# An expert stage whose experts follow one another without a seam: two buffers of split tokens, and prompt tokens turned as full tiles

## The chip, the core and the metric

The kernel runs on one core of one Trainium2 chip. The metric is the device time of one execution in microseconds (us). Three runs of the kernel before gave 3706.44, 3706.96 and 3714.54 us, with a median of 3706.96 us.

The engines are named as in the profile: PE is TensorE (matmuls), PEld its weight loads, DVE is VectorE, ACT is ScalarE, POOL is GpSimd, and SP is the engine that issues most DMAs.

## The reference, cut to what matters

One encoder layer is applied to 512 prompt tokens and 1024 sample tokens with shared weights: a mixer (attention and convolution), and then a mixture of 16 experts in which each expert takes its best tokens. The change touches only the second part:

```python
def expert_choice_ffn(h, w_router, w_gate, w_up, w_down):
    cap = max(1, EC_FACTOR * n // N_EXPERTS)       # 64 prompt, 128 sample tokens
    hf = h.reshape(n, D)
    aff = jax.nn.softmax((hf @ w_router).astype(jnp.float32), axis=-1)
    g, idx = lax.top_k(aff.T, cap)
    xe = hf[idx]
    hid = jax.nn.silu(jnp.einsum('ecd,edf->ecf', xe, w_gate)) * jnp.einsum('ecd,edf->ecf', xe, w_up)
    ye = jnp.einsum('ecf,efd->ecd', hid, w_down) * g[..., None].astype(h.dtype)
    y = jnp.zeros((n, D), h.dtype).at[idx.reshape(-1)].add(ye.reshape(-1, D))
```

Everything is float32. D is 1024, the hidden width of an expert is 2816, which is 22 tiles of 128 rows, and an expert's tokens are 192 columns (64 prompt, 128 sample).

## The kernel before, in words

The function `experts` writes out the work of each engine as its own program. The order on each engine is the order of the code, and semaphores tie the engines together. No planner or scheduler is involved.

To keep float32 accuracy on the fast matmul path, each operand is split into a high part (rounded by ACT) and a low part (the rest, subtracted by DVE). Three products are summed.

**A step.** An expert has 22 steps, one for each tile i of its hidden width. On PE a step is `gate_up(e, i)`: 16 pairs of matmuls (L1204 with the high weights over 384 columns, L1206 with the low weights over 192 columns). With two steps of delay (`BEHIND = 2`) comes `down(e, i-2)`: 10 matmuls of 512 columns (L1221 to L1225), which gather the expert's output in the PSUM tile `psY` over all 22 steps. ACT copies part of the gate/up result out of PSUM (`low`, L1337), DVE adds the other part (`gu`, L1428), ACT takes the silu (L1341), DVE multiplies (`hid`, L1433), and both split the result (`hs`, L1348, L1438, L1439). In between, ACT and DVE split the weights of gate and up two steps ahead (`AHEAD = 2`; L1308, L1394) and the weights of down for this step (L1318, L1399). So in each step DVE ends with `lo_down` (L1399).

**The tokens of the next expert.** POOL gathers the rows of the next expert's tokens from HBM into `xg_p` (64 rows) and `xg_s` (128 rows), L1242 and L1244. In steps 6, 8, ... 20 of an expert, PE turns an eighth k of them each time, ahead of that step's gate/up: one transpose of 128 rows (L1172) and one of 64 rows (L1173). ACT moves each eighth into `xst` (L1297). The split buffer `xe` exists once, so it is filled in one piece for all eighths when the last step's gate/up has been read: one ACT instruction of 1536 elements (L1322) and one on DVE (L1404), at the end of step 21.

**Between two experts.** PE runs `gate_up(e, 21)`, then `down` 19, 20 and 21 in a row, and only then `gate_up(e+1, 0)`. The first `down` of the next expert, after its third gate/up, starts `psY` anew, so it waits until the output of the expert before has been taken out (`y_scaled`, L1216). That output work is `y_out` on DVE (L1409 to L1418, four passes in all with `yhalf` on ACT, L1328), done ahead of step 0 of the next expert. POOL then scatters the rows with an add (L1257, L1259), waits until they have landed, copies the index lists (L1249 to L1252) and gathers the tokens of the expert after (L1242, L1244).

**Loops.** On PE, expert 0 is written out and experts 1 to 15 are a hardware loop of 15 rounds (`pe.Fori(1, EXPERTS)`, L1235), so its end jumps back 14 times. On ACT and DVE, experts 0 and 15 are written out, with a loop of 14 rounds between (L1369, L1460).

Of the kernel before, what the change touches and what calls it, by code (L numbers as in the profile page):

```python
# [1058 lines left out]
def experts(nc, A, sem, sb, ps, y_d, ada_d, xhat_d, ident, modv, a2, affT):  # L1059
# [8 lines left out]
    HS = 3  # L1068
# [14 lines left out]
    x_turned, xs_ready, x_hi, x_lo = sem("x_turned"), sem("xe_staged"), sem("xe_hi"), sem("xe_lo")  # L1083
    y_half, y_sent_s, y_sent_p, y_scaled = sem("y_half"), sem("scattered_s"), sem("scattered_p"), sem("y_scaled")
# [9 lines left out]
    with ExitStack() as c:  # L1094
# [38 lines left out]
        with nc.Block() as block:  # L1133
# [30 lines left out]
            def _(pe):  # L1164
# [5 lines left out]
                def turn(k, bank):  # L1170

                    pe.transpose(psG[:, bank, 2 * CAP:2 * CAP + P], xg_s[:, :].rearrange("p (d k) -> p k d", k=KD)[:, k, :], ident[:, :])  # L1172
# [4 lines left out]
                pe.wait_ge(sel_ready, 1)  # L1177
                pe.wait_ge(g_loaded_s, 16)
# [6 lines left out]
                def gate_up(e, i, first):  # L1185
# [6 lines left out]
                    if turned_in(i) is not None:  # L1192
# [6 lines left out]
                    for m in range(2):  # L1199
                        pe.wait_ge(gu_lo, 2 * n + m + 1)  # L1200
                        bank = psG[:, 2 * a + m]
                        for k in range(KD):
                            wh, wl = (w[:, a, m, k * P:(k + 1) * P] for w in (w_hi, w_lo))
                            pe.matmul(bank[:, 0:2 * CAP], wh, xe[:, k, :, :].rearrange("p a b -> p (a b)"), start=(k == 0), stop=False,  # L1204
                                      skip_group_check=True)
                            mm = pe.matmul(bank[:, 0:CAP], wl, xe[:, k, 0, :], start=False, stop=(k == KD - 1),  # L1206
# [3 lines left out]
                def down(e, i, first):  # L1210
# [7 lines left out]
                    s_hi, pp, s_lo = (hs[:, i % HS, at * P:(at + 1) * P] for at in range(3))  # L1218
# [74 lines left out]
            def _(act):  # L1293
# [36 lines left out]
                def step(e, i, first, last):  # L1330
# [7 lines left out]
                    if nxt and i < FT - 1:  # L1338
                        hi(*nxt, 0)
# [182 lines left out]
```

## Time and profile before

| what | value |
|---|---|
| median of three runs | 3706.96 us |
| span of the profiled execution | 3698.8 us |
| rest of a run beside that span | 8.2 us, if the profiled execution took the median |
| expert stage, first gate/up to last down | 1149.8 to 3680 us |
| PE busy, whole span | 3374.2 us, 91% |
| DVE busy | 2386.4 us, 65% |
| ACT busy | 1936.3 us, 52% |
| POOL busy | 530.3 us, 14% |
| share of the DMA engines on the weight queue | 47.9% |
| granted TensorE clock, mean | 0.952 |

The page of the profile gives no separate time for the profiled execution, only its span, from its first to its last instruction. All times inside it are counted from the span's start. The expert stage is two thirds of it. There PE is busy in nearly all slices, so idle time of the other engines costs nothing as long as PE does not wait for them. A record of PE ends where the profiler models its end, so the start-to-start distance of matmuls tells more than their durations. PEclk is the granted clock: 1.00 is 2.4 GHz and 0.50 is 1.2 GHz.

### The profile page before, as it was taken

How to read it: one execution, taken by the hardware profiler on the slowest of the kernel's cores; microseconds unless marked ns; L12 is line 12 of the kernel's file. 1: busy time of each engine (PE TensorE's matmuls, PEld its weight loads, DVE VectorE, ACT ScalarE, POOL GpSimd, SP SyncE). 2: the span in 40 equal slices, each digit the busy share in tenths (PEclk: the TensorE clock that was granted, in tenths of full speed). 3: DMA queues.
4: the chain of work that ended last, by engine and by line, in shares of the span. 5: the costliest groups of instructions: out<-in, count | busy, mean ns of one | idle time of the engine just before them, and what ended most of it. 6: DMA issues, size and time to landing. Idle time of an engine off the chain costs nothing. (4 is left out here: it accounts for less than half of the span.)

```text
span 3698.8 us, 50959 instructions
## 1 busy us (share of the span) xinstructions
PE 3374.2 (91%) x18510; PEld 2905.0 (79%) x18510; DVE 2386.4 (65%) x3652; ACT 1936.3 (52%) x3202; POOL 530.3 (14%) x461
## 2 busy tenths in 40 slices
PE   8597878698936999999999999999999999999998
PEld 1385656356825999999989999999999989999997
DVE  0277884474465677676766766677676766767675
ACT  0622322364524566565655655566566656655664
POOL 0079993000001000000100100000010101001010
PEclk9698889799967999999999999999999999999999
DMA  8301111704234475665757656475665756656572
GB/s 320 121 26 49 49 36 56 247 35 160 106 133 154 180 282 214 247 222 205 256 205 256 221 218 245 184 278 212 249 226 201 256 210 251 234 204 247 198 260 89
DMA packets 143349, 697.42 MB, mean 189 GB/s; under 512 B 12388, under 2 KB 39524, under 8 KB 119588
## 3 DMA queue, kind: packets, MB, share of 16 engines
q1 hardware_dynamic: 131620, 659.75, 47.9%
q0 software_dynamic: 7392, 25.96, 3.1%
q10 hardware_dynamic: 4132, 8.65, 0.7%
q8 instruction: 169, 2.77, 0.3%
q14 instruction: 36, 0.29, 0.0%
HBM read 656.51 MB, written 37.80 MB: 188 GB/s over the span
## 5 line engine op out<-in xcount | busy, mean ns | idle before, releaser
L1204 PE MATMUL psG<-xe,w_gu_hi_part 128*128 128x384 f32 x5632 | 1647.3, 362 | 28.5 <-DVE w_gu_lo_part L1394 24.4
L1206 PE MATMUL psG<-xe,w_gu_lo_part 128*128 128x192 f32 x5632 | 1415.1, 251 | 0.0
L1204 PEld LDWEIGHTS psG<-xe,w_gu_hi_part 128*128 128x128 f32 x5632 | 1061.7, 189 | 50.3 <-DVE w_gu_lo_part L1394 30.2
L1206 PEld LDWEIGHTS psG<-xe,w_gu_lo_part 128*128 128x128 f32 x5632 | 1079.7, 192 | 7.1
L1394 DVE TENSOR_TENSOR w_gu_lo_part<-raw_gu,w_gu_hi_part 128x1024 fp32r<-128x1024 f32 x704 | 859.6, 1223 | 117.6 <-ACT w_gu_hi_part L1308 117.6
L1308 ACT ACTIVATE w_gu_hi_part<-raw_gu 128x1024 fp32r<-128x1024 f32 x704 | 741.4, 1056 | 12.8 <-DMA raw_gu<-in_w_gu 12.8
L1428 DVE TENSOR_TENSOR gu<-psG,low 128x384 f32<-128x384 f32 x352 | 196.1, 557 | 640.4 <-ACT low L1337 640.4
L1399 DVE TENSOR_TENSOR w_dn_lo_part<-raw_dn,w_dn_hi_part 128x1024 fp32r<-128x1024 f32 x352 | 431.3, 1225 | 9.6 <-ACT w_dn_hi_part L1318 9.6
L1337 ACT ACTIVATE low<-psG 128x384 f32<-128x384 f32 x352 | 172.8, 491 | 449.7 <-PE psG L1206 449.7
L1318 ACT ACTIVATE w_dn_hi_part<-raw_dn 128x1024 fp32r<-128x1024 f32 x352 | 368.9, 1048 | 0.0
L1257 POOL DMA_INDIRECT out<-ye,inow x16 | 26.3, 1643 | 2269.8 <-DVE yp L1418 2269.8
L1297 ACT ACTIVATE xst<-psG,modv,a 128x128 f32<-128x128 f32 (+1 forms) x272 | 102.5, 428 | 462.4 <-PE psG L1206 395.3
L1221 PE MATMUL psY<-w_dn_hi_part,hs 128*128 128x512 f32 x704 | 284.9, 405 | 2.3
L1224 PE MATMUL psY<-w_dn_hi_part,hs 128*128 128x512 f32 x704 | 276.5, 393 | 0.0
L1222 PE MATMUL psY<-w_dn_lo_part,hs 128*128 128x512 f32 x704 | 276.1, 392 | 0.0
L1223 PE MATMUL psY<-w_dn_hi_part,hs 128*128 128x512 f32 x704 | 275.4, 391 | 0.0
L1225 PE MATMUL psY<-w_dn_lo_part,hs 128*128 128x512 f32 x704 | 275.2, 391 | 0.0
L575 DVE SCALAR_TENSOR_TENSOR acc<-u,convp,acc 128x1024 f32<-128x1024 f32 x120 | 226.4, 1887 | 3.7
L508 PE MATMUL psZ<-h_hi,w_hi 128*128 128x512 f32 x480 | 208.1, 434 | 13.8 <-DVE w_lo L338 8.1
L583 POOL TENSOR_TENSOR acc<-acc,prod 128x512 f32<-128x512 f32 x120 | 211.2, 1760 | 10.0
L1348 ACT ACTIVATE hs<-hid 128x192 fp32r<-128x192 f32 x352 | 129.1, 367 | 141.7 <-DVE hid L1433 140.8
L509 PE MATMUL psZ<-h_lo,w_hi 128*128 128x512 f32 x480 | 193.2, 403 | 0.0
(159 smaller groups left out, 3962.5 us busy)
## 6 DMA issues: line engine op xcount, KB each, us to landing
raw_gu<-in_w_gu SPq DMA_DIRECT2D x176, 2048.0 KB, 8.7
raw_dn<-in_w_down SPq DMA_DIRECT2D x176, 1024.0 KB, 8.7
aw<-in_ada_w SPq DMA_DIRECT2D x12, 2048.0 KB, 8.7
bias<-in_bias SPq DMA_DIRECT2D x8, 1536.0 KB, 10.8
w_raw<-in_w_in SPq DMA_DIRECT2D x20, 512.0 KB, 5.4
qk_d<-zg SPq DMA_DIRECT2D x8, 768.0 KB, 3.7
qk<-qk_d SPq DMA_DIRECT2D x8, 768.0 KB, 12.0
out<-wo_raw SPq DMA_DIRECT2D x12, 512.0 KB, 2.6
```

The source lines that it names most:

```text
L575: eng.scalar_tensor_tensor(out=dst, in0=src, scalar=convp[:, j, t:t + 1], in1=dst, op0=ALU.mult, op1=ALU.add).then_inc(counter, 1)
L1204: pe.matmul(bank[:, 0:2 * CAP], wh, xe[:, k, :, :].rearrange("p a b -> p (a b)"), start=(k == 0), stop=False, skip_group_check=True)
L1206: mm = pe.matmul(bank[:, 0:CAP], wl, xe[:, k, 0, :], start=False, stop=(k == KD - 1), skip_group_check=True)
L1221: pe.matmul(psY[:, h, :], s_hi, wh, start=st, stop=False)
L1222: pe.matmul(psY[:, h, :], s_hi, wl, start=False, stop=False)
L1223: pe.matmul(psY[:, h, :], s_lo, wh, start=False, stop=en)
L1224: pe.matmul(psY[:, 2 + h, :], pp, wh, start=st, stop=False)
L1225: mm = pe.matmul(psY[:, 2 + h, :], pp, wl, start=False, stop=en)
L1308: act.activation(w_hi[:, i % 2, m], raw_gu[:, s, m, i % 2], ACT.Copy).then_inc(gu_hi, 1)
L1318: act.activation(d_hi[:, i % 2], raw_dn[:, s, i % 2], ACT.Copy).then_inc(dn_hi, 1)
L1394: dve.tensor_tensor(w_lo[:, i % 2, m], raw_gu[:, (i // 2) % RING_GU, m, i % 2], w_hi[:, i % 2, m].bitcast(F32), ALU.subtract).then_inc(gu_ ...
L1399: dve.tensor_tensor(d_lo[:, i % 2], raw_dn[:, (i // 2) % RING_DN, i % 2], d_hi[:, i % 2].bitcast(F32), ALU.subtract).then_inc(dn_lo, 1)
```

## The change

Five edits, all in `experts`.

1. `xe` becomes two buffers, one being read while the other is filled. The split of the tokens into high and low is done eighth by eighth in the steps that turn them (`xsplit(e, k, at)`), on ACT after the second weight split of the step and on DVE after `hs`. Nothing of it is left at the end of step 21.
2. The last two `down` of an expert are no longer run in a row. `down(e-1, 20)` comes after `gate_up(e, 0)`, and `down(e-1, 21)` after `gate_up(e, 1)`. The ring `hs` gets a fourth buffer for that. The output work (`yhalf`, `y_out`) therefore moves from ahead of step 0 to behind step 1.
3. The loops on PE, ACT and DVE run over pairs of experts, since the buffer of `xe` and of `hs` must be known in the code: on PE experts 0 and 15 are written out and the loop has 7 rounds, so its end jumps back 6 times.
4. `xg_p` gets 128 rows. The rows 64 to 127 are set to zero once, and the prompt tokens are turned by a transpose of 128 rows.
5. The last expert no longer gathers, turns or stages tokens that nobody uses (before, the tokens of expert 0 were fetched again): 8 pairs of transposes fewer.

```diff
-    HS = 3
+    HS = 4
...
-        xg_p = sb(c, "xg_p", [CAP_P, D])
+        xg_p = sb(c, "xg_p", [P, D])
...
-        xe = sb(c, "xe", [P, KD, 2, CAP], F32R)
+        xe = sb(c, "xe", [P, 2, KD, 2, CAP], F32R)
...
-                    pe.transpose(psG[:, bank + 1, 2 * CAP:2 * CAP + CAP_P], xg_p[:, :].rearrange("p (d k) -> p k d", k=KD)[:, k, :],
-                                 ident[0:CAP_P, 0:CAP_P]).then_inc(x_turned, 1)
-
+                    for tile, b in ((xg_s, bank), (xg_p, bank + 1)):
+                        mm = pe.transpose(psG[:, b, 2 * CAP:2 * CAP + P],
+                                          tile[:, :].rearrange("p (d k) -> p k d", k=KD)[:, k, :], ident[:, :])
+                    mm.then_inc(x_turned, 1)
...
-                        pe.wait_ge(x_lo, e + 1)
+                        pe.wait_ge(x_lo, KD * (e + 1))
...
-                def expert(e, first):
-                    for i in range(FT + BEHIND):
-                        if i < FT:
-                            gate_up(e, i, first)
+                def expert(e, at, first, last):
+                    for i in range(FT):
+                        gate_up(e, i, at, first, last)
                         if i >= BEHIND:
-                            down(e, i - BEHIND, first)
-                expert(0, True)
-                with pe.Fori(1, EXPERTS) as e:
-                    expert(e, False)
+                            down(e, i - BEHIND, at, first)
+                        elif not first:
+                            down(e - 1, FT - BEHIND + i, 1 - at, False)
+                expert(0, 0, True, False)
+                with pe.Fori(1, EXPERTS - 1, 2) as e:
+                    expert(e, 1, False, False)
+                    expert(e + 1, 0, False, False)
+                expert(EXPERTS - 1, 1, False, True)
+                for i in range(FT - BEHIND, FT):
+                    down(EXPERTS - 1, i, 1, False)
...
-                def xsplit(e):
-                    act.wait_ge(xs_ready, KD * (e + 1))
-                    act.activation(xe[:, :, 0, :], xst[:, :, :], ACT.Copy).then_inc(x_hi, 1)
+                def xsplit(e, k, at):
+                    act.wait_ge(xs_ready, KD * e + k + 1)
+                    act.activation(xe[:, at, k, 0, :], xst[:, k, :], ACT.Copy).then_inc(x_hi, 1)
...
-                    if nxt and i < FT - 1:
+                    if nxt:
                         hi(*nxt, 1)
-                    back = last_user(i, HS, FT)
-                    if not (first and back < 0):
-                        act.wait_ge(dn_done, e * FT + back + 1)
+                    if k is not None:
+                        xsplit(e + 1, k, 1 - at)
+                    if not (first and i < HS):
+                        act.wait_ge(dn_done, n - HS + 1)
...
-                    if nxt and i == FT - 1:
-                        xsplit(e + 1)
-                        hi(*nxt, 0)
-                        hi(*nxt, 1)
...
-                def xsplit(e):
-                    dve.wait_ge(x_hi, e + 1)
-                    dve.tensor_tensor(xe[:, :, 1, :], xst[:, :, :], xe[:, :, 0, :].bitcast(F32), ALU.subtract).then_inc(x_lo, 1)
+                def xsplit(e, k, at):
+                    dve.wait_ge(x_hi, KD * e + k + 1)
+                    dve.tensor_tensor(xe[:, at, k, 1, :], xst[:, k, :], xe[:, at, k, 0, :].bitcast(F32), ALU.subtract).then_inc(x_lo, 1)
...
+                    if turned_in(i) is not None and not last:
+                        xsplit(e + 1, turned_in(i), 1 - at)
                     lo_down(e, i)
-                    if nxt and i == FT - 1:
-                        xsplit(e + 1)
-                        lo(*nxt, 0)
-                        lo(*nxt, 1)
-
-                def expert(e, first, last):
+
+                def expert(e, at, first, last):
                     for i in range(FT):
-                        if i == 0 and not first:
+                        step(e, i, at, first, last)
+                        if i == BEHIND - 1 and not first:
                             y_out(e - 1)
-                        step(e, i, first, last)
```

The order of the instructions shows two places of this. The first is VectorE between expert 0 and expert 1. Before, with `xe` as the split tokens, `w_gu_lo_part` as the low weights of gate and up, and `ye` and `yp` as the output rows of the sample and the prompt tokens:

```order
L1399 TENSOR_TENSOR w_dn_lo_part<-raw_dn,w_dn_hi_part 128x1024 [waits w_dn_hi]
L1404 TENSOR_TENSOR xe<-xst,xe 128x8x192 [waits xe_hi]
L1394 TENSOR_TENSOR w_gu_lo_part<-raw_gu,w_gu_hi_part 128x1024 [waits w_gu_hi] x2
L1460 UNCONDITIONAL_BRANCH
L1460 ISA
L1409 ISA [waits pool_steps]
L1409 COPY gnow<-gsel 128x1
L1410 ISA
L1410 COPY gnow<-gsel 128x1
L1411 ISA
L1412 REGISTER_ALU [waits y_scaled]
L1413 SCALAR_TENSOR_TENSOR ye<-psY,gnow,gate 128x1024 [waits down_done]
```

And in the changed kernel, the end of step 1 of expert 1 on the same engine (L1410 is `lo_down`, L1424 to L1429 the output of expert 0, and L1439 the beginning of step 2):

```order
L1450 TENSOR_TENSOR hs<-hid,hs 128x128
L1410 TENSOR_TENSOR w_dn_lo_part<-raw_dn,w_dn_hi_part 128x1024 [waits w_dn_hi]
L1419 ISA
L1420 ISA [waits pool_steps]
L1420 COPY gnow<-gsel 128x1
L1421 ISA
L1421 COPY gnow<-gsel 128x1
L1422 ISA
L1424 SCALAR_TENSOR_TENSOR ye<-psY,gnow,gate 128x1024 [waits down_done,y_scaled]
L1427 TENSOR_TENSOR yp<-psY,yp 64x1024 [waits y_half]
L1428 REGISTER_ALU
L1429 SCALAR_TENSOR_TENSOR yp<-yp,gnow,gate 64x1024 [waits y_scaled]
```

The output work has moved behind two whole steps of the next expert, and the split of the tokens and the doubled weight split have left the seam.

The second place is PE. Before, at the end of expert 0, the last `down` matmuls stand directly ahead of the first gate/up of expert 1:

```order
L1225 MATMUL psY<-w_dn_lo_part,hs 128x512
L1235 UNCONDITIONAL_BRANCH
L1235 ISA
L1191 ISA [waits xe_lo]
L1200 ISA [waits gate_up_summed]
L1204 MATMUL psG<-xe,w_gu_hi_part 128x384 [waits w_gu_lo]
```

In the changed kernel, `down` 20 of expert 0 stands between the first and the second gate/up of expert 1 (L1206 and L1208 are the gate/up matmuls here, L1223 to L1227 those of `down`):

```order
L1208 MATMUL psG<-xe,w_gu_lo_part 128x192
L1215 ISA
L1223 MATMUL psY<-w_dn_hi_part,hs 128x512 [waits hid_lo,w_dn_lo]
L1224 MATMUL psY<-w_dn_lo_part,hs 128x512
L1225 MATMUL psY<-w_dn_hi_part,hs 128x512
L1226 MATMUL psY<-w_dn_hi_part,hs 128x512
L1227 MATMUL psY<-w_dn_lo_part,hs 128x512
```

The wait for `y_scaled` stays where it was, ahead of `down` 0 and behind the third gate/up. What moved is that one gate/up now lies between the last `down` of an expert and that wait, where there were three.

## Rows read from the trace of the kernel before

**Rows 1.** waits in the expert stage: who waited for whom, us in total, times, longest us
```profile
PE psG L1204 <- DVE w_gu_lo_part L1394: 24.4, 14, 2.2
PEld psY L1221 <- DVE w_dn_lo_part L1399: 9.1, 16, 0.6
```

**Rows 2.** timeline, PE, expert 4 to 5: start us, duration us, engine, line, operation
```profile
1936.18 0.39 PE L1225 MATMUL psY<-w_dn_lo_part,hs 128*128 128x512 f32 x1
1937.05 0.39 PE L1222 MATMUL psY<-w_dn_lo_part,hs 128*128 128x512 f32 x1
...
1938.88 0.39 PE L1225 MATMUL psY<-w_dn_lo_part,hs 128*128 128x512 f32 x1
1941.17 0.44 PE L1204 MATMUL psG<-xe,w_gu_hi_part 128*128 128x384 f32 x1 [1.90 <-DVE w_gu_lo_part L1394]
1941.45 0.25 PE L1206 MATMUL psG<-xe,w_gu_lo_part 128*128 128x192 f32 x1
```

**Rows 3.** timeline, PE and VectorE, expert 0 to 1
```profile
1307.73 0.39 PE L1225 MATMUL psY<-w_dn_lo_part,hs 128*128 128x512 f32 x1
...
1308.13 0.25 PE L1206 MATMUL psG<-xe,w_gu_lo_part 128*128 128x192 f32 x1
...
1307.33 2.35 DVE L1394 TENSOR_TENSOR w_gu_lo_part<-raw_gu,w_gu_hi_part 128x1024 fp32r<-128x1024 f32 x2
```

**Rows 4.** DMA queues between 1618 and 1626 us: kind, packets, MB, share of 16 engines
```profile
q8 instruction: 2, 0.03, 1.9%
```

**Rows 5.** timeline, PE, around a pair of turning matmuls in expert 5
```profile
2008.08 0.40 PE L1225 MATMUL psY<-w_dn_lo_part,hs 128*128 128x512 f32 x1
...
2009.05 0.25 PE L1206 MATMUL psG<-xe,w_gu_lo_part 128*128 128x192 f32 x1
```

**Rows 6.** timeline, PE, projection stage: four 128-row transposes between matmuls of 512 columns
```profile
573.27 0.60 PE L488 MATMUL psS<-ident,sqz 128*128 128x128 f32 x4
...
573.94 0.39 PE L509 MATMUL psZ<-h_lo,w_hi 128*128 128x512 f32 x1
```

**Rows 7.** timeline, a step without turning on three engines
```profile
1903.51 0.49 ACT L1337 ACTIVATE low<-psG 128x384 f32<-128x384 f32 x1 [1.79 <-PE psG L1206]
...
1907.93 1.23 DVE L1399 TENSOR_TENSOR w_dn_lo_part<-raw_dn,w_dn_hi_part 128x1024 fp32r<-128x1024 f32 x1
...
1931.80 0.41 PE L1221 MATMUL psY<-w_dn_hi_part,hs 128*128 128x512 f32 x1
...
1932.00 0.49 ACT L1337 ACTIVATE low<-psG 128x384 f32<-128x384 f32 x1 [1.79 <-PE psG L1206]
```

**Rows 8.** timeline, VectorE, the output of expert 4
```profile
1938.48 2.35 DVE L1394 TENSOR_TENSOR w_gu_lo_part<-raw_gu,w_gu_hi_part 128x1024 fp32r<-128x1024 f32 x2
...
1943.53 1.28 DVE L1418 SCALAR_TENSOR_TENSOR yp<-yp,gnow,gate 64x1024 f32<-64x1024 f32 x1
```

**Rows 9.** timeline, ScalarE, first copy of low in experts 1 and 5
```profile
1312.68 0.49 ACT L1337 ACTIVATE low<-psG 128x384 f32<-128x384 f32 x1 [3.50 <-PE psG L1206]
...
1947.62 0.49 ACT L1337 ACTIVATE low<-psG 128x384 f32<-128x384 f32 x1 [7.29 <-PE psG L1206]
```

**Rows 10.** PE idle, projection stage: timeline; busy times of a window, granted clock third last
```profile
459.62 0.50 PE L508 MATMUL psZ<-h_hi,w_hi 128*128 128x512 f32 x1 [2.98 <-DVE w_lo L338]
...
461.00:464.00 3.00, 3.00 (x9) 2.33 (x8) 2.93 (x3) 0.00 (x0) 2.92 (x2) 0.53 0.00 0
```

**Rows 11.** timeline, GpSimd, scatter and gather of two experts, and landing of the gather
```profile
1945.65 1.60 POOL L1257 DMA_INDIRECT out<-ye,inow  x1 [139.56 <-DVE yp L1418]
...
1960.76 1.11 POOL L1244 DMA_INDIRECT xg_s<-xhat_d,inow  x1 [0.30 <-issue]
...
3369.54 1.60 POOL L1257 DMA_INDIRECT out<-ye,inow  x1 [140.81 <-DVE yp L1418]
...
3387.20 0.98 POOL L1244 DMA_INDIRECT xg_s<-xhat_d,inow  x1 [0.30 <-issue]
...
DMA to landing us min/median/max: 5.1/5.6/10.9
```

More of the change, by code:

```diff
@@ L1183, in _, with gate_up @@
                     turn(k, 2 * (k % 2))
-                def gate_up(e, i, first):
+                def gate_up(e, i, at, first, last):
                     a = i % 2
@@ L1267, in _, with expert @@
                 gather(0)
-                def expert(e, nxt):
+                def expert(e, last):
                     pool.wait_ge(g_loaded_s, 16 * (e + 1))
@@ L1328, in yhalf, with step @@
                     act.activation(yp[:, :], psY[CAP_P:P, 2:4, :].rearrange("p a b -> p (a b)"), ACT.Copy).then_inc(y_half, 1)
-                def step(e, i, first, last):
+                def step(e, i, at, first, last):
                     a = i % 2
@@ L1366, in _ @@
                     stage(k, 2 * (k % 2))
-                xsplit(0)
-                expert(0, True, False)
-                with act.Fori(1, EXPERTS - 1) as e:
-                    expert(e, False, False)
-                expert(EXPERTS - 1, False, True)
+                for k in range(KD):
+                    xsplit(0, k, 0)
+                expert(0, 0, True, False)
+                with act.Fori(1, EXPERTS - 1, 2) as e:
+                    expert(e, 1, False, False)
+                    expert(e + 1, 0, False, False)
+                expert(EXPERTS - 1, 1, False, True)
                 yhalf(EXPERTS - 1)
@@ L1419, in y_out, with step @@
                                              in1=gate2[0:CAP_P, 0, :], op0=ALU.mult, op1=ALU.mult).then_inc(y_scaled, 1)
-                def step(e, i, first, last):
+                def step(e, i, at, first, last):
                     a = i % 2
@@ L1440, in step, with expert @@
                                       ALU.subtract).then_inc(hid_lo, 1)
+                    if turned_in(i) is not None and not last:
+                        xsplit(e + 1, turned_in(i), 1 - at)
                     lo_down(e, i)
-                    if nxt and i == FT - 1:
-                        xsplit(e + 1)
-                        lo(*nxt, 0)
-                        lo(*nxt, 1)
-                def expert(e, first, last):
+                def expert(e, at, first, last):
                     for i in range(FT):
-                        if i == 0 and not first:
+                        step(e, i, at, first, last)
+                        if i == BEHIND - 1 and not first:
                             y_out(e - 1)
-                        step(e, i, first, last)
                 dve.wait_ge(sel_ready, 1)
@@ L1457, in _ @@
                         lo(0, i, m)
-                xsplit(0)
-                expert(0, True, False)
-                with dve.Fori(1, EXPERTS - 1) as e:
-                    expert(e, False, False)
-                expert(EXPERTS - 1, False, True)
+                for k in range(KD):
+                    xsplit(0, k, 0)
+                expert(0, 0, True, False)
+                with dve.Fori(1, EXPERTS - 1, 2) as e:
+                    expert(e, 1, False, False)
+                    expert(e + 1, 0, False, False)
+                expert(EXPERTS - 1, 1, False, True)
                 y_out(EXPERTS - 1)
```

49 lines of the change are left out of this document (27 added, 22 removed).

## The prediction

> **What bounds the kernel now.** Read the busy shares first. PE is busy for 91% of the span and in nearly every slice of the expert stage, DVE for 65%, ACT for 52%. A change of this stage is worth what it does to PE's own work and to PE's waits. So the second view is who PE and its weight loads waited for in the stage [rows 1]. Two waits stand there, and both lie at the seam between experts: 14 before the first gate/up, and 16 before the last `down`. The third view is the timeline of PE at such a seam.
>
> At the seam from expert 4 to 5 PE leaves its last `down` matmul at 1938.88 and reaches the first low matmul of gate/up at 1941.45, 2.57 us later [rows 2]. At the seam from 0 to 1 the same two matmuls lie 1308.13 − 1307.73 = 0.40 us apart [rows 3]. So the stall costs 2.17 us there, against 1.90 us of idle time in the row: idle plus 0.27. The profile names DVE's low weights (L1394) as releaser. That can't be: from 0 to 1 the same DVE pair ran from 1307.33 to 1309.68, and PE had already started. The code agrees, since gate/up 0 needs the weights split in step 20. What differs is that PE's loop jumps back at the later seams. There are 14 jumps and 14 such waits, and none at the one seam without a jump. In the 8 us around such a seam two packets of instructions were fetched [rows 4]. I take the jump as the cause. The Trainium skill (Runtime: NRT & Kernel Launch, Instruction fetch mechanics) says that a taken branch whose target isn't in the fetched window waits for a DMA. The rows agree.
>
> **The change part by part.** I count changes of the span of 3698.8 us. The page gives no other time for the profiled execution, so I add the sum to the median, 8.2 us above that span.
>
> *Fewer jumps.* The loop of pairs jumps back 6 times, not 14. PE's idle for this cause is 24.4 us over 14 [rows 1]. With 24.4/14 + 0.27 = 2.0 us each, 8 jumps less give −16.1. The six that are left keep their price. ACT and DVE bodies double too. Should their jumps now stall as PE's does, PE's own stall of 2 us at the same place and the 1 to 2 us by which they run ahead hide it.
>
> *Down 21 at once after down 20.* Here PE waits for the low down weights of step 21: 1937.05 − 1936.18 = 0.87 us over what is else two pitches of 0.23 (1937.05 to 1938.88 is eight) [rows 2]. That is 0.41 each, and 15 of 16 go, since the last expert still ends so: −6.2.
>
> *Full transposes.* A turning pair now puts 2009.05 − 2008.08 = 0.97 us between the last `down` and the first low matmul, where 0.40 is normal: 0.57 a pair [rows 3, 5]. Full tiles back to back are to be seen in the projection stage: four of them take 573.94 − 573.27 − 0.23 = 0.44 us, 0.11 each [rows 6]. Two would cost 0.22, which saves 0.35 on each of 120 pairs: −42. The bounds are 0, if a full tile costs in this place what half a pair costs now, and −48, if it costs nearly nothing beside the weight loads (0.17). I take −42, since rows 6 show the same kind of instruction, start to start. The 8 pairs of the last expert go altogether: 8 × 0.57 = −4.6. One more rule speaks against this edit. The Trainium skill (TensorE: Matmul & The Clock Gate, Part 4: PE-mode transpose) gives about 275 ns for a 128×128 transpose in a kernel. By that two cost 0.55, and the term would be −2. The row of four disagrees with it.
>
> *The splits by eighths.* ACT's and DVE's large instructions leave the seam. Each eighth is one short instruction in a step in which both have idle time, ACT 1.8 us before `low` [rows 7]. Nothing, but for the start of the stage, where the chain of both is shortened by some 0.6 us: −0.6. If the cover were gone, 0.3 us in each of 120 steps would be 36.
>
> *The output work moves: a new wait.* PE's `down` 0 waits for `y_scaled`, and behind it the whole of PE's queue. Count from the moment at which PE begins `down` 21, right behind gate/up 1. ACT's `low` starts 0.20 us later (1931.80 and 1932.00) [rows 7]. DVE's step 1 ends with L1399, 1907.93 + 1.23 − 1903.51 = 5.65 us after `low` [rows 7]. Only then comes the output work: from 1940.83 (the end of the row at 1938.48) to 1944.81 (1943.53 + 1.28), 3.98 us [rows 8]. So `y_scaled` comes after 9.83 us. PE meanwhile has `down` 21, 10 × 0.23 = 2.3 us, and gate/up 2, 1312.68 − 0.20 − 1307.96 (1307.73 + 0.23) = 4.52 us [rows 3, 9], together 6.8. PE waits 3.0 us and pays 0.1 more to start again (the idle and restart at a jump show 0.27 over the idle) : 3.1 us at each of 15 seams, +47. Before, three gate/ups covered the same work. The bounds are 2.5 and 3.5 us each, 38 to 53.
>
> *The gather moves with it.* POOL scatters after the output, waits, and gathers the next tokens. From the end of the output (1944.81) to the scatter are 0.84 us, from there to the gather of `xg_s` 15.1 us in one expert and 17.7 in the slowest, and 5.6 more to landing: 21.5 to 24.1 us [rows 11]. PE needs them in step 6. From the end of the output it has four `down` and three gate/ups before that, and the restart: 9.2 + 13.6 + 0.2 = 23.0 us. Before, the output ended some 15 us earlier in the expert, so there was plenty. Now about half of the seams are late by up to 1.1 us: +4 (0 to 12).
>
> *The clock.* After the seam at 1941 the first gate/up is complete (`low`) 1947.62 − 1941.17 = 6.45 us after its start; undisturbed it is 4.72 [rows 9]. Less the restart this is 1.6 us, and the granted clock was at its lower level of 1.2 GHz in between. This happened at 4 of 14 jumps, of which the row shows one: 6.4 us now. The new wait leaves PE idle for about 2.9 us. One idle stretch of 2.98 us in the projection stage was followed by the lower clock [rows 10]. I take half of 15, and 6 × 4/14 for the jumps: 9.2 falls, 14.8 us, so +8.4 (bounds −3.8 and +20.4).
>
> The sum: −16.1 − 6.2 − 42 − 4.6 − 0.6 = −69.5; +47 + 4 + 8.4 = +59.4; together −10. Added to the median of 3706.96 that is 3697 us. Two large terms nearly cancel.
>
> **The rivals.**
>
> *B, the clock holds.* If the new wait is just too short for a fall, the clock gives −3.8 and the gather +5.4: −69.5 + 47 + 5.4 − 3.8 = −21, 3686 us. For it: only 4 of 14 stalls of 2 us fell. Against it: the stretch of 2.98 us.
>
> *C, it falls each time.* +20.4 and only +1 for the gather, which the slow stretch covers: −1, 3706 us.
>
> *D, the gather becomes the bound (the slower side).* Place: PE's first transpose in step 6. It decides once the tokens land on average 24.2 us or more after the output, 1.2 us over PE's 23.0, since each microsecond beyond costs 15. For it: scatter and gather share the DMA engines with weight loads, and would now meet others. Against it: in the rows the slowest is 24.1. At 2.4 us of lateness on average it gives −10 − 4 + 36 = +22, 3729 us.
>
> *E, full transposes are no cheaper in this place:* a pair keeps its 0.57 us, and 42 us of the gain go: −10 + 42 = +32, 3739 us. It could be so if the 0.57 comes from leaving and entering the split matmuls, and not from the half tile. The row of four, which also stands between split matmuls, speaks against it. The Trainium skill's 275 ns (TensorE: Matmul & The Clock Gate, Part 4) would bring the same.
>
> *F, the profile's releaser is right and not the jump.* Then all 14 stalls vanish, 6 × 2.0 more and less clock loss: 3684 us. The seam from 0 to 1 speaks against it.
>
> *G, the output wait doesn't bite*, since PE is late or DVE early by 3 us: 3640 us. No row is that far off.
>
> *H, a jump over twice the body costs twice:* +12, 3709 us.
>
> **How the numbers follow.** Chances: forecast 0.38 (its own range 3690 to 3706), B 0.20, C 0.13, D 0.10, E 0.06, F 0.05, G 0.03, H 0.05. What can be told from no change is 0.2%, 7.4 us. Faster, below 3699.6, are B, F, G and 0.23 of the forecast: 0.51. Same are the rest of the forecast, most of C and half of H: 0.29. Slower are D, E and the remains: 0.20. The range 3680 to 3722 leaves out G, the outer part of D, and E: about 0.2 with the tails.
>
> **What would show it.** In the changed profile PE's idle rows before gate/up at a seam should be 6, not 14, each 1.3 to 2.2 us. A new wait for the output on DVE (now L1429) should stand before `down` 0, 15 times, about 2.9 us each. From the last `down` to the low matmul over a turning pair should be 0.6 us, not 0.97. The wait for `xg_s` in step 6 should be short and in about half of the experts. Wrong would I be if that last wait is 2 us or more (D), if the transposes keep their 0.57 (E), or if `down` 0 doesn't wait (G).

## The result, and the profile after

| | kernel before | changed kernel |
|---|---|---|
| median of the runs of one comparison, us | 3708.54 (3706.44 to 3714.54) | 3738.54 (3733.91 to 3741.58) |
| ratio, 95% interval | 1 | 1.008 (1.0064 to 1.0097) |
| span of the profiled execution, us | 3698.8 | 3736.8 |
| mean granted clock | 0.952 | 0.943 |

The change makes the kernel 0.8% slower. The forecast of 3697 us had the wrong sign, and the time lies above its range. A second comparison gave 3729.11 against 3705.74 us, ratio 1.006 (1.004 to 1.0081).

The waits of TensorE in the expert stage, in the changed kernel; columns as in [rows 1]:

```profile
PE psY L1223 <- DVE yp L1429: 41.3, 15, 2.8
PE psG L1206 <- issue: 20.4, 6, 3.8
PE psG L1174 <- DMA xg_s<-xhat_d,inow: 15.4, 12, 1.7
PE psG L1206 <- DVE xe L1415: 3.4, 1, 3.4
PE psG L1208 <- issue: 1.1, 2, 0.8
PEld psY L1223 <- DVE w_dn_lo_part L1410: 0.6, 1, 0.6
```

Against [rows 1], 15 of the 16 waits for the low down weights are gone. The 14 rows before gate/up have become 6, but their sum fell from 24.4 us to 20.4 only. Two waits are new: the output (`yp`) and the gathered tokens (`xg_s`).

The output wait, at the seam from expert 0 to 1, on the timeline of PE, and then the ends of gate/up as ScalarE's first copy shows them:

```profile
1324.82 0.36 PE L1206 MATMUL psG<-xe,w_gu_hi_part 128*128 128x384 f32 x1
1325.02 0.25 PE L1208 MATMUL psG<-xe,w_gu_lo_part 128*128 128x192 f32 x1
1328.01 0.80 PE L1223 MATMUL psY<-w_dn_hi_part,hs 128*128 128x512 f32 x1 [2.75 <-DVE yp L1429]
```

```profile
1318.44 0.49 ACT L1349 ACTIVATE low<-psG 128x384 f32<-128x384 f32 x1 [2.48 <-PE psG L1208]
1325.30 0.49 ACT L1349 ACTIVATE low<-psG 128x384 f32<-128x384 f32 x1 [1.44 <-PE psG L1208]
1336.58 0.49 ACT L1349 ACTIVATE low<-psG 128x384 f32<-128x384 f32 x1 [3.41 <-PE psG L1208]
1343.41 0.49 ACT L1349 ACTIVATE low<-psG 128x384 f32<-128x384 f32 x1 [2.45 <-PE psG L1208]
```

A step takes 6.86 us (1325.30 − 1318.44); the one with the wait takes 11.28, which is 4.42 more. A seam at which the clock held took 9.83. So the wait itself costs 2.97 us, and the slower clock behind it about 1.4. The matmul behind the wait lasts 0.80 us instead of 0.40. The granted clock behind two such waits (columns: window; its length; busy us of PE, weight loads, VectorE, ScalarE, GpSimd; clock; DMA share; GB/s):

```profile
1329.00:1331.00 2.00, 2.00 (x6) 1.58 (x5) 2.00 (x4) 1.13 (x2) 2.00 (x1) 0.50 0.92 379
1489.00:1491.00 2.00, 2.00 (x7) 1.62 (x7) 1.32 (x3) 0.55 (x2) 1.70 (x2) 0.50 1.12 420
```

0.50 is the 1.2 GHz level. Between 1170 and 3600 us the changed kernel has 17 such stretches, at 12 of the 15 output waits and 5 of the 6 jumps and nowhere else, against 4 in the kernel before. Three of the 17 lasted twice as long as the rest and cost twice as much (the step with the wait then took 12.67 us, 2.84 over the 9.83, not 11.28, 1.45 over). Below, stretches are counted by length, a double one as two: 20 against 4.

What answers to the seam of [rows 2], the only kind with a jump left (PE, expert 2 to 3):

```profile
1624.10 0.40 PE L1226 MATMUL psY<-w_dn_hi_part,hs 128*128 128x512 f32 x1
1624.33 0.40 PE L1227 MATMUL psY<-w_dn_lo_part,hs 128*128 128x512 f32 x1
1627.92 0.53 PE L1206 MATMUL psG<-xe,w_gu_hi_part 128*128 128x384 f32 x1 [3.19 <-issue]
1628.26 0.36 PE L1208 MATMUL psG<-xe,w_gu_lo_part 128*128 128x192 f32 x1
```

From the last `down` to the first low matmul are 3.93 us, where [rows 2] have 2.57. The releaser is now given as "issue": PE waited for nothing that the profile shows. PE's instruction queue in the 10.9 us up to the gate/up behind the jump, in the kernel before (1930.2 to 1941.1) and in the changed one (1617 to 1627.9), as packets, MB and share of 16 engines:

```profile
q8 instruction: 1, 0.02, 0.9%
```

```profile
q8 instruction: 2, 0.03, 1.2%
```

The packet next to the jump starts at 1937.85 in the kernel before, 1.03 us ahead of the last `down` matmul, and at 1625.12 in the changed one, 0.79 us behind it. The second packet of the changed kernel starts at 1621.40.

Around a turning pair, what answers to [rows 5]:

```profile
2013.08 0.40 PE L1227 MATMUL psY<-w_dn_lo_part,hs 128*128 128x512 f32 x1
2013.32 0.27 PE L1174 MATMUL psG<-ident,xg_s 128*128 128x128 f32 x1
2013.42 0.27 PE L1174 MATMUL psG<-ident,xg_p 128*128 128x128 f32 x1
2013.45 0.42 PE L1206 MATMUL psG<-xe,w_gu_hi_part 128*128 128x384 f32 x1
2013.71 0.25 PE L1208 MATMUL psG<-xe,w_gu_lo_part 128*128 128x192 f32 x1
```

2013.71 − 2013.08 = 0.63 us. The prediction asked for 0.6.

The gather, what answers to [rows 11]: GpSimd's rows, the wait in step 6, and the landing over all experts.

```profile
1973.75 2.23 POOL L1264 DMA_INDIRECT out<-ye,inow  x1 [147.02 <-DVE yp L1429]
...
1989.55 0.96 POOL L1251 DMA_INDIRECT xg_s<-xhat_d,inow  x1 [0.30 <-issue]
```

```profile
1999.26 0.38 PE L1174 MATMUL psG<-ident,xg_s 128*128 128x128 f32 x1 [1.66 <-DMA xg_s<-xhat_d,inow]
```

```profile
DMA to landing us min/median/max: 4.3/9.4/10.7
```

Scatter to gather is 15.8 us here (15.1 and 17.7 in the two experts of [rows 11]). Over all experts its median fell from 17.0 to 15.2 us. The landing took 9.4 us in the median, not 5.6.

**Where the 38.0 us of span went** (3736.8 − 3698.8):

| piece | read as | us |
|---|---|---|
| before the stage, code that is the same | first transpose of the top values at 1126.7, not 1118.4; in the attention stage the clock was at 1.2 GHz for 68.3 us, not 54.6 | +8.3 |
| from there to the first gate/up | 30.2 us, not 31.4 | −1.2 |
| full transposes | 0.575 − 0.235 = 0.34 × 120 pairs | −40.8 |
| 8 pairs of the last expert | as in the prediction | −4.6 |
| wait for low down weights | 15 of 16 gone | −6.2 |
| jumps | 20.4 + 1.1 + 6 × 0.27 = 23.1, not 28.2 | −5.1 |
| output wait | 15 × 2.97 | +44.6 |
| gather wait | 15.4 + 12 × 0.27 to start again | +18.6 |
| slower clock | 20 − 4 = 16 more stretches by length, × 1.5 | +24 |
| sum | | +37.6 |

The 0.235 is two neighbouring steps, one with turning (7.00 + 6.95 = 13.95 us), less two without (13.72). The 1.5 lies between the 1.4 here and the 1.6 at [rows 9]. The first piece probably doesn't belong to the change. The same transpose started at 1113.5 and 1114.1 in two kernels below that have the changed kernel's code up to there (experiments 2 and 3), but at 1126.0 when the changed kernel ran again. With the code of the kernel before up to there it started at 1126.2 in experiment 8, and at 1129.3 in experiment 1. So single profiles differ by up to 16 us before the stage begins, and the medians below carry some of that.

### The profile page after: what moved, and what is told of

Its sections match the earlier page's. It is cut to its first block, busy times and chain, and to the rows that moved or that the text cites. A ratio compares the mean times of both kernels' runs of the same rounds, so it can differ in the third digit from the quotient of the medians.

```text
span 3736.8 us, 51239 instructions
## 1 busy us (share of the span) xinstructions
PE 3360.7 (90%) x18494; PEld 2913.5 (78%) x18494; DVE 2386.4 (64%) x3764; ACT 1935.6 (52%) x3298; POOL 524.5 (14%) x456
## 4 chain that ended last, share of the span: by engine, by line
PE 55%; DMA 5%; DVE 4%; issue 3%; POOL 2%; ACT 1%; POOLq 0%; DVEq 0%; ACTq 0%
PE psG L1206 25%; PE psG L1208 12%; PE psY L1223 4%; PE psY L1226 4%; PE psY L1224 4%; PE psY L1225 4%; PE psY L1227 3%; DMA xg_s<-xhat_d,inow 3%; DMA out<-yp,inow 2%; PE psG L1174 1%; DVE w_gu_lo_part L1405 1%; POOL out L1264 1%; DVE idxu L1394 1%; DVE affT L1396 1%; DVE yp L1429 1%
## 5 line engine op out<-in xcount | busy, mean ns | idle before, releaser
L1206 PE MATMUL psG<-xe,w_gu_hi_part 128*128 128x384 f32 x5632 | 1647.6, 362 | 23.7 <-issue 20.4
L1208 PE MATMUL psG<-xe,w_gu_lo_part 128*128 128x192 f32 x5632 | 1417.3, 252 | 1.1 <-issue 1.1
L1206 PEld LDWEIGHTS psG<-xe,w_gu_hi_part 128*128 128x128 f32 x5632 | 1068.0, 190 | 38.5 <-issue 24.4
L1208 PEld LDWEIGHTS psG<-xe,w_gu_lo_part 128*128 128x128 f32 x5632 | 1084.8, 193 | 10.1
L1439 DVE TENSOR_TENSOR gu<-psG,low 128x384 f32<-128x384 f32 x352 | 196.1, 557 | 665.1 <-ACT low L1349 665.1
L1410 DVE TENSOR_TENSOR w_dn_lo_part<-raw_dn,w_dn_hi_part 128x1024 fp32r<-128x1024 f32 x352 | 430.9, 1224 | 22.8 <-ACT w_dn_hi_part L1329 22.8
L1264 POOL DMA_INDIRECT out<-ye,inow x16 | 35.0, 2189 | 2331.0 <-DVE yp L1429 2331.0
L1223 PE MATMUL psY<-w_dn_hi_part,hs 128*128 128x512 f32 x704 | 289.4, 411 | 41.4 <-DVE yp L1429 41.3
L1226 PE MATMUL psY<-w_dn_hi_part,hs 128*128 128x512 f32 x704 | 281.7, 400 | 0.0
L1224 PE MATMUL psY<-w_dn_lo_part,hs 128*128 128x512 f32 x704 | 280.9, 399 | 0.0
L1225 PE MATMUL psY<-w_dn_hi_part,hs 128*128 128x512 f32 x704 | 279.9, 398 | 0.0
L1227 PE MATMUL psY<-w_dn_lo_part,hs 128*128 128x512 f32 x704 | 279.2, 397 | 0.0
L510 PE MATMUL psZ<-h_hi,w_lo 128*128 128x512 f32 x480 | 192.6, 401 | 0.0
```

The costliest lines, as they stand in the source:

```text
L1206: pe.matmul(bank[:, 0:2 * CAP], wh, xe[:, at, k, :, :].rearrange("p a b -> p (a b)"), start=(k == 0), stop=False, skip_group_check=True)
L1208: mm = pe.matmul(bank[:, 0:CAP], wl, xe[:, at, k, 0, :], start=False, stop=(k == KD - 1), skip_group_check=True)
L1223: pe.matmul(psY[:, h, :], s_hi, wh, start=st, stop=False)
L1224: pe.matmul(psY[:, h, :], s_hi, wl, start=False, stop=False)
L1225: pe.matmul(psY[:, h, :], s_lo, wh, start=False, stop=en)
L1226: pe.matmul(psY[:, 2 + h, :], pp, wh, start=st, stop=False)
```

## The experiments

Each edit is given against the kernel named. Ratios are against runs of the kernel before on the same chip.

**1. Only the full tile, in the kernel before.** Of the change, this takes the prompt tile of 128 rows and nothing else.

```diff
-        xg_p = sb(c, "xg_p", [CAP_P, D])
+        xg_p = sb(c, "xg_p", [P, D])
-                    pe.transpose(psG[:, bank + 1, 2 * CAP:2 * CAP + CAP_P], ... ident[0:CAP_P, 0:CAP_P])
+                    pe.transpose(psG[:, bank + 1, 2 * CAP:2 * CAP + P], ... ident[:, :])
```

> The kernel before with one edit: xg_p has 128 rows, of which 64 are zero, and is turned by a transpose of 128 rows. Theory (a full tile is cheap, and the changed kernel's slowness comes from its seams): from the last down matmul to the first low matmul over a turning pair 0.63 us instead of 0.97, so 0.34 us on each of 136 pairs, about -44 us against the kernel before (3708.5), that is 3665 us. Rival (the full tile is no cheaper once the seams are as before, since the half tile's drain lay beside something else): 3708 us and 0.97 us in the trace.

Measured: 3659.5 us, ratio 0.9875 (0.985 to 0.990). By the ratio the transposes are worth 46 us alone. In the profiles, from the first transpose of the top values to the end, it is 44.3 us (2580.4 and 2536.1). In the steps there are 128 pairs (the expectation's 136 counts 8 more at the start of the stage), and 128 × 0.34 = 44. The term stands. The waits at the jumps are those of before:

```profile
PE psG L1207 <- DVE w_gu_lo_part L1399: 24.4, 14, 2.2
```

**2. The changed kernel with the seam of before.** `down` 20 and 21 stay in their own expert, and the output work comes ahead of step 0. Pairs of experts in one loop body, eighths and full tiles stay.

```diff
-                        elif not first:
-                            down(e - 1, FT - BEHIND + i, 1 - at, False)
+                    for i in range(FT - BEHIND, FT):
+                        down(e, i, at, first)
...
-                        step(e, i, at, first, last)
-                        if i == BEHIND - 1 and not first:
+                        if i == 0 and not first:
                             yhalf(e - 1)
+                        step(e, i, at, first, last)
```

> The changed kernel with the old seam: down 20 and 21 stand behind down 19 in the same expert, and the output work stands ahead of step 0 of the next expert on ACT and DVE. The two buffers of xe, the splits by eighths, the full tiles and the loop over pairs stay. Theory A (the moved output work made PE wait at down 0, the clock fell there and the gather came late): against the changed kernel's 3738.5 the wait for y_scaled goes (-45), the gather's wait (-19), the clock falls at it (-21), and 6 us come back for the low down weights of step 21. Theory A1 (a jump is dearer there because only 10 down matmuls stand ahead of it, so that PE's sequencer has not run ahead): with 30 of them the idle at the 6 jumps goes back from 3.6 to 1.8 us, with fewer clock falls, -18 more: 3642 us. Rival A2 (a jump is dearer because the loop's body is twice as long): idle stays 3.6 us, 3660 us. Rival B (the fault is in the eighths or the pairs, not in the seam): stays near 3738 us.

Measured: 3652.95 us, ratio 0.9863 (0.9841 to 0.9886). PE's waits in the stage:

```profile
PE psY L1223 <- DVE w_dn_lo_part L1408: 16.9, 15, 1.1
PE psG L1206 <- issue: 10.8, 6, 2.3
```

The waits for output and gather are gone, and one stretch at the lower clock is left. The jumps cost 10.8/6 = 1.8 us of idle, as in the kernel before, though the body is as long as in the changed kernel. So the length of the body alone doesn't make a jump cost 3.4 us: that came with the moved `down`. The time is near the expectation's A1, but its reason (30 `down` matmuls ahead of the jump) isn't shown by this, as the account of the prediction below says. The miss of 11 us against the expectation is the first row. Step 21 turns no tokens, but it now splits gate and up weights ahead of the down weights, which the kernel before did at its end. So the last down weights are ready later than PE wants them.

**3. PE written out, in the changed kernel.** No loop on PE, so no jump.

```diff
-                with pe.Fori(1, EXPERTS - 1, 2) as e:
-                    expert(e, 1, False, False)
-                    expert(e + 1, 0, False, False)
+                for e in range(1, EXPERTS - 1):
+                    expert(e, e % 2, False, False)
```

> The changed kernel with PE's program written out for all 16 experts: no loop on PE, so no jump back. Theory (the 6 idle stretches before gate/up 0, 3.6 us each, and the clock falls behind them are the jump and nothing else): -23 for the idle and restarts, -11 for the clock: 3704 us, no idle row before gate/up at the seams. Rival (they are a wait for another engine, as the profile of the kernel before had it): the idle stays, 3738 us. Waits for the output and for the gather stay in either case.

Measured: 3712.78 us, ratio 1.002 (1.0003 to 1.0037).

```profile
PE psY L1223 <- DVE yp L1428: 45.2, 15, 4.1
PE psG L1174 <- issue: 19.0, 13, 2.8
```

The second row is the wait for the gathered tokens, by its place in step 6. The waits for "issue" before gate/up are gone, which confirms the jump. The gain is 22 us by the ratios: 23.1 for the jumps and about 6 for the clock (16 stretches by length are left of 20), less 8 us by which the other two waits grew. It misses the expectation by 9.

**4. The gather early, in the changed kernel.** GpSimd gathers the tokens of expert e + 2 ahead of the scatter of e.

```diff
-                        lists(e + 1, 1)
-                        pool.wait_ge(idx_now, 2 * e + 3)
+                        lists(e + 2, 1)
+                        pool.wait_ge(idx_now, 2 * e + 4)
                         pool.sem_inc(pool_steps)
-                        gather(e + 1)
+                        gather(e + 2)
```

> The changed kernel with one edit on POOL: the tokens of expert e+2 are gathered as soon as those of expert e+1 have been turned (step 20 of expert e), ahead of the scatter of expert e, not behind it. Theory (the gather's wait in step 6 comes from the chain output, scatter, lists, gather, which moved 15 us back with the output): the wait of PE for xg_s is gone, -19 us: 3720 us; the waits for y_scaled stay 2.75 us. Rival (the landing is slow because of the weight transfers, wherever the gather stands): the wait stays, 3738 us.

Measured: 3730.9 us, ratio 1.0075 (1.0052 to 1.0099): against 3738.5 a gain of 8 us at most, and none that the intervals tell apart.

```profile
PE psY L1223 <- DVE yp L1438: 41.2, 15, 2.8
PE psG L1206 <- issue: 20.7, 6, 3.8
PE psG L1208 <- issue: 5.3, 5, 1.4
```

The gather wait is gone, but the clock fell behind all 15 output waits and all 6 jumps, 24 stretches by length instead of 20, and a second short wait behind the jumps rose from 1.1 to 5.3 us. Together these return some 10 us of the 18.6. Landing still takes 9.5 us in the median here, so standing behind the scatter isn't what slows it.

**5. Full tile and PE written out, in the kernel before.** The edits of 1 and 3 on the kernel before, without its seam being touched.

```diff
-                with pe.Fori(1, EXPERTS) as e:
+                for e in range(1, EXPERTS):
                     expert(e, False)
```

> The kernel before with full transposes (as in the first experiment, 3659.5 us) and PE's 16 experts written out, so that PE never jumps back. Theory (the 14 waits that the profile puts down to DVE's low weights are jumps): 24.4 us of idle and 3.8 for the restarts go, and most of the clock falls behind them (9 low stretches in that profile, 1.6 us each, so up to 14): -28 to -42, 3618 to 3632 us, no idle before gate/up 0. Rival (they wait for DVE's low weights): 3659 us and the same 14 rows.

Measured: 3627.58 us, ratio 0.9797 (0.978 to 0.9813), as expected. No stretch of the stage is at the lower clock, and PE waits at no seam.

**6. One `down` moved instead of two.** In the kernel of 4, `down` 20 stays in its expert, only `down` 21 goes behind gate/up 0, the output work follows step 0, and PE is written out.

```diff
-                        elif not first:
-                            down(e - 1, FT - BEHIND + i, 1 - at, False)
+                        elif i == 0 and not first:
+                            down(e - 1, FT - 1, 1 - at, False)
+                    down(e, FT - BEHIND, at, first)
...
-                        if i == BEHIND - 1 and not first:
+                        if i == 0 and not first:
                             y_out(e - 1)
```

> A version meant to keep what is good in the change. The changed kernel, but down 20 stays in its own expert, only down 21 goes behind gate/up 0 of the next, and the output work stands behind step 0, so that two gate/ups (9.1 us) and not one cover it; the gather is ahead of the scatter; PE is written out. Theory: the output ends 9.8 us after PE begins down 21, PE needs it after 2.3 + 9.1 = 11.4 us, so no wait; no jump, no gather wait, no wait for the low down weights, hardly a clock fall: against the changed kernel -45 -23 -19 -6 (of the clock 20 falls x 1.6 = 32) = 3738 - 119 = 3619 us, and some 6 us less than before with full tiles and PE written out. Rival (the output work in any place behind a step makes PE wait or disturbs DVE): a wait for y_scaled of over 1 us at each seam, 3650 us or more.

Measured: 3640.02 us, ratio 0.9827 (0.9811 to 0.9843), 21 us above the expectation.

```profile
PE psY L1223 <- DVE yp L1437: 12.0, 6, 2.0
PE psG L1206 <- DVE xe L1423: 3.4, 1, 3.4
PE psG L1206 <- DVE w_gu_lo_part L1413: 2.5, 4, 0.8
```

PE waits 2.0 us at 6 seams and not at 15, and 6 is the number of jumps that ScalarE and VectorE still make. ScalarE itself stands idle 6 times, 4.3 us each, for nothing that the profile shows:

```profile
ACT w_gu_hi_part L1327 <- issue: 25.8, 6, 4.7
```

**7. The output ahead of the low down weights, in the changed kernel.** VectorE does the output work before the last split of step 1.

```diff
+                    if i == BEHIND - 1 and not first:
+                        y_out(e - 1)
                     lo_down(e, i)
```

> The changed kernel with one edit on DVE: the output work stands ahead of the split of the down weights of step 1, not behind it. It ends 1.2 us earlier. Theory (the wait at down 0 is DVE's order): idle there goes from 2.75 to 1.55 us, -18 us, and the stall is then as short as a jump's in the kernel before, which drew a clock fall in 4 of 14: from about 12 falls to 4, -13 more: 3707 us. Rival 1 (falls do not depend on the length of the idle stretch between 1.5 and 2.8 us): -18 only, 3720 us. Rival 2 (the wait is for the scatter or for ACT, not for DVE's order): 3738 us.

Measured: 3702.44 us, ratio 1.0001 (0.9988 to 1.0014).

```profile
PE psY L1223 <- DVE yp L1429: 23.4, 15, 1.6
PE psG L1174 <- DMA xg_s<-xhat_d,inow: 20.1, 14, 1.7
PE psG L1206 <- issue: 20.0, 6, 4.2
```

One VectorE instruction of 1.2 us moved takes 1.2 us off each of the 15 waits, 17.9 together. By the ratios the gain is 29 us. The rest is the clock, 8 stretches by length instead of 20 (about 18 us), less some 5 us by which the gather wait grew. All 8 lie at 5 of the 6 jumps. None of the 15 waits of 1.6 us was followed by a fall, while 12 of the 15 of 2.8 us were in the changed kernel.

**8. PE written out alone, in the kernel before.** The edit of 5 without the full tile.

```diff
-                with pe.Fori(1, EXPERTS) as e:
+                for e in range(1, EXPERTS):
                     expert(e, False)
```

> The kernel before with PE's 16 experts written out and nothing else. Theory (14 jumps): -28 for idle and restarts, -6 for 4 clock falls: 3674 us, and the idle of 24.4 us before gate/up is gone. Rival (waits for DVE's low weights): 3708 us, 14 rows of idle as before.

Measured: 3671.74 us, ratio 0.991 (0.989 to 0.9929). What is left of PE's waits in the stage, and the seam of [rows 2] again:

```profile
PE psG L1204 <- DVE xe L1404: 4.1, 1, 4.1
```

```profile
1938.59 0.39 PE L1225 MATMUL psY<-w_dn_lo_part,hs 128*128 128x512 f32 x1
1938.82 0.33 PE L1204 MATMUL psG<-xe,w_gu_hi_part 128*128 128x384 f32 x1
1939.08 0.36 PE L1204 MATMUL psG<-xe,w_gu_hi_part 128*128 128x384 f32 x1
```

Nothing that VectorE does was changed, and the 14 waits that [rows 1] put down to it are gone. The profile's releaser was wrong, the jump is the cause, and it cost 33 us by the ratio. The parts, 28.2 of waits and 4 × 1.6 of slow clock, make 34.6.

**9. All three engines written out, in the kernel of 6.**

```diff
-                with act.Fori(1, EXPERTS - 1, 2) as e:
-                    expert(e, 1, False, False)
-                    expert(e + 1, 0, False, False)
+                for e in range(1, EXPERTS - 1):
+                    expert(e, e % 2, False, False)
```

and the same for VectorE.

> The version with the half interleaving (3640.0 us), with ACT and DVE written out as well, so that no engine but SP and POOL jumps back. There, 6 waits of 2.0 us for the output stood at every second seam, where DVE's and ACT's loops jump, and 4 waits of 0.4 to 0.8 us for the low weights. Theory (those waits are DVE's and ACT's own jumps, since their doubled bodies no longer stay fetched): all 10 go (-14.5 us, -1.6 for restarts) and the 4 clock falls with them (-6): 3618 us, under the 3627.6 us of the kernel before with full tiles and PE written out. Rival (the output work behind step 0 is late by itself at every second seam): the 6 waits stay, 3640 us.

Measured: 3615.44 us, ratio 0.9756 (0.9738 to 0.9773), near the 3618 expected. It beats both kernels, and no stretch of the stage is at the lower clock. Of PE's waits in the stage only the one at its start is left:

```profile
PE psG L1206 <- DVE xe L1422: 3.4, 1, 3.4
```

The instruction queue whose packets change with the loops of ScalarE and VectorE, first in experiment 6 and then here (packets, MB, share of 16 engines):

```profile
q14 instruction: 112, 0.92, 0.1%
```

```profile
q14 instruction: 77, 0.63, 0.0%
```

So the waits of 6 were jumps again, of the two engines that PE waits for. In the kernel before, with one expert per body, this queue moved 36 packets.

**10. The changed kernel again, unaltered.** This asks whether the 8.3 us before the stage belong to the change.

> The changed kernel, unaltered. In its first profile the expert stage began 7 us later than in the kernel before, since TensorE's clock rose later in the attention stage, whose code is the same. Theory (that differs from execution to execution and has nothing to do with the change): first transpose of the top values anywhere between 1113 and 1127 us, median of the runs within 3725 to 3741 us, and the expert stage itself as long as in the first profile, 2610 us from that transpose to the end, within 4 us. Rival (the change's code, of which more is fetched or laid out elsewhere, delays the earlier stages): 1126.7 us again in each profile of the changed kernel.

Measured: 3729.11 us, ratio 1.006 (1.004 to 1.0081). The transpose of the top values started at 1126.0, late again. From it to the end were 2614.5 us, against 2610.1 in the first profile, a little more than the 4 us allowed; by length it has 24 stretches at the lower clock, not 20. PE's waits repeat:

```profile
PE psY L1223 <- DVE yp L1429: 41.3, 15, 2.8
PE psG L1206 <- issue: 21.4, 6, 4.2
PE psG L1174 <- DMA xg_s<-xhat_d,inow: 14.7, 11, 1.7
```

By this run alone the late start could belong to the changed kernel. Experiments 2 and 3 have its code up to that point and started at 1113.5 and 1114.1, and experiment 8, with the code of the kernel before up to there, at 1126.2. So I take it for a difference between profiles that the change doesn't make. With two profiles of the changed kernel that isn't settled; it concerns 8 of the 38 us.

## Why the prediction was wrong

**Right.** *Full transposes:* 0.34 us a pair against the 0.35 forecast. The pair costs 0.235 and not 0.22. Experiment 1 gave 46 us for the edit alone, on 128 pairs (128 × 0.34 = 44). Rival E falls. The Trainium skill (TensorE: Matmul & The Clock Gate, Part 4: PE-mode transpose) gives about 275 ns for a 128×128 transpose in one kernel. The duration column of this trace agrees (0.27 us), but two starts lie 0.10 us apart, and only that enters the sum. *The wait for low down weights* went as said. *The output wait* was forecast at 3.1 us, 15 times, and is 2.97: rival G falls. *The jump as cause:* [rows 1] name another releaser, and experiments 3, 5 and 8 show that none of it stays once PE has no jump. Rival F falls.

**Wrong, the jumps: "The six that are left keep their price".** They cost 3.85 us instead of 2.0, so −5 in place of −16. The step gave a jump one price, whatever stands around it. That the price moved with the `down` matmuls is shown: experiment 2 has the same doubled body with the old seam, and idle is 1.8 us. Rival H had the sign but the wrong mechanism.

How the moved `down` raise it stays open. In the kernel before, the fetch next to the jump started 0.9 to 1.1 us before the last `down` matmul at 13 of 14 jumps, and gate/up followed 2.7 to 3.5 us after the fetch. In the changed kernel it started 0.5 to 1.2 us after the last one at all six, and gate/up followed 2.8 to 3.0 us later. So the fetch comes later; it doesn't take longer. It looks as if 30 matmuls in PE's queue were a cover and 10 were none, but the rows speak against that. In the kernel before PE was held by the low down weights ahead of `down` 21, so that only 10 matmuls were left from there to the jump, and in the changed kernel there are 10 as well:

```profile
1936.71 0.50 PE L1221 MATMUL psY<-w_dn_hi_part,hs 128*128 128x512 f32 x1
```

```profile
1622.23 0.41 PE L1223 MATMUL psY<-w_dn_hi_part,hs 128*128 128x512 f32 x1
```

The fetch starts 1.14 us after the first of these (1937.85), and 2.89 us after the second (1625.12). What else differs is one more fetch, at 1621.40. At each of the six jumps one starts 3.7 to 4.7 us before the fetch next to the jump, while in the kernel before and in experiment 2 none stands within 8 us. That where the loop's end lies in the fetched code sets the price is a rival that no run here separates from the cover.

**Wrong in size, the gather: +4, measured +18.6.** The chain from output to gather was right (0.84 + 15.8 us). The failed number is the landing, taken from the kernel before at 5.6 us and now 9.4: the price of a transfer was carried to another moment. Standing behind the scatter isn't the reason: ahead of it, experiment 4 shows 9.5 us. Experiments 1, 2, 5 and 8, all with the old seam, have 5.8 to 6.2. While the gather of `xg_s` was under way, the weight queue moved 157 GB/s in the median of the kernel before and 253 in the changed one (153 to 188 in the five kernels with the old seam, 232 to 295 in the others). That fits a sharing of the DMA engines with the weight loads; no run tests it by itself. Tokens land 26.0 us after the output in this expert (0.84 + 15.8 + 9.4; the median is 25.7), beyond D's point of 24.2. Of D's 36 us half came; the slow stretches behind the output wait gave the tokens 1.4 us more.

**Wrong in size, the clock: "I take half of 15", +8.4, measured +24.** 12 of 15 output waits were followed by a fall, and 5 of 6 jumps in place of 2 of 6; three of the falls lasted twice as long. The jumps follow from the first error: idle of 3.4 us instead of 1.7. For the waits, one stretch of 2.98 us in the trace had fallen [rows 10] and I still took a half; C, at 12 of 15, was nearly right. Experiment 7 is the test of it: behind 15 waits of 1.6 us there is no fall, and those that are left lie at the jumps.

**In sum.** The terms for what goes were right within 2 us, but for the jumps (11 short). Of what comes, the output wait was 2 too dear, the gather 15 and the clock 16 too cheap. Together these are about 40 us, the distance from −10 to the 29 us that are left of the sum without the piece before the stage. The prediction had a rival for each of the three, D, C and H, but as cases that exclude each other. They came together, and the longer idle at the jumps raised the clock's term too. The range was built from one at a time.

## What to carry to other kernels

Before moving work past a loop's end, take the price of its jump as one that can change with the work around it: here 2.0 us became 3.85. Writing PE's loop out, with nothing else changed, was worth 33 us. When a large saving (41 us) comes with a new wait, price the wait with the fall of the clock behind it and with the transfers that it shifts to another moment. And split the change: the full tile alone and PE written out gave 3627.6 us, where the whole change lost what the tile had won. Half of the move, with the gather early and all three engines written out, gave 3615.4 us, so the idea wasn't wrong, but its place and its jumps cost more than it saved.

## What the runs showed of the hardware

- From the start of the instruction fetch next to a jump of PE's loop to the next matmul were 2.7 to 3.5 us. Idle was 1.7 to 1.8 us with three `down` ahead of the jump (14 and 6 jumps) and 3.4 us with one, where the fetch started later; why is open. In the kernel before, the profile named VectorE's low weights as its releaser, elsewhere "issue".
- ScalarE and VectorE showed no cost for a jump over one expert (experiments 5 and 8). Over two, ScalarE stood idle 4.3 us at each jump, and each jump cost PE a wait of 2.0 us where it waits for their output (experiment 6), and written out none (experiment 9).
- Idle of 2.8 us was followed by the 1.2 GHz level in 12 of 15 cases (11 and 15 of 15 in experiments 10 and 4), idle of 3.4 us in 5 of 6, of 2.0 us in 4 of 6 (experiment 6), of 1.7 us in 4 of 14, of 1.6 us in none of 15 (experiment 7). A fall cost 1.4 to 1.6 us, and twice that when it lasted twice as long.
- A 128-row and a 64-row transpose between the matmuls of two steps cost 0.575 us together, two of 128 rows 0.235, although they move more rows.
- An indirect gather of 128 rows landed in 5.6 to 6.2 us (medians of the five kernels with the old seam) and in 8.6 to 9.9 us (the seven others).
